# Mask matmuls behind the scores and a new split of the probability copies, in the attention stage of a two-layer trunk

## The reference, cut to what matters

```python
def sink_attend(qb, keys, values, masks, sinks):
    for kk, m in zip(keys, masks):
        s = jnp.einsum('bqhgd,bkhd->bhgqk', qb, kk).astype(jnp.float32) * scale
        if m is not None:
            s = jnp.where(m, s, -jnp.inf)
        parts.append(s)
    sink = ...                                   # one learned logit for each head
    p = jax.nn.softmax(jnp.concatenate(parts + [sink], axis=-1), axis=-1)
    ...                                          # out = sum over the parts of p @ v

def one_block(b):                                # 8 blocks of 128 queries
    qb = ...                                     # 128 queries, 16 heads of 64
    kb, vb = ...                                 # 384 keys and values around the block
    mask = (jnp.abs(qi[:, None] - offs[None, :]) <= WINDOW) & ((kpos >= 0) & (kpos < L))[None, :]
    return sink_attend(qb, (kb, k_ctx), (vb, v_ctx), (mask, None), sinks)
```

## Time and profile before

| | |
|---|---|
| median of 3 runs | 3098.88 us (3095.15 to 3099.98) |
| profiled execution, its own time | 3098.88 us |
| its span, first to last instruction | 3096.9 us |
| TensorE busy over the span | 2845.7 us (92%) |
| VectorE, ScalarE, GpSimd busy | 1610.1, 645.7, 502.0 us (52%, 21%, 16%) |
| mean granted TensorE clock | 0.960 |
| attention stage, first mask matmul to last division | 285.0 to 582.8 us |

### The profile page before, as it was taken

One profiled execution on the slowest core, in us unless ns is written; L12 is line 12 of the kernel. 1 busy time (PEld: TensorE's weight loads), 2 busy tenths in 40 slices (PEclk: granted clock), 3 DMA queues, 4 the chain that ended last, 5 costly groups with the idle time before them and its releaser, 6 DMA issues. The chain is left out here.

```text
span 3096.9 us, 40772 instructions
## 1 busy us (share of the span) xinstructions
PE 2845.7 (92%) x15266; PEld 1384.1 (45%) x15267; DVE 1610.1 (52%) x3256; ACT 645.7 (21%) x1161; POOL 502.0 (16%) x396
## 2 busy tenths in 40 slices
PE   5998999999799999999999588997999999999983
PEld 2444666544344444444443364443434444444430
DVE  3885555466545454545453355564544545454536
ACT  0112555201111121212121240011111111111110
POOL 0000000111022222222221111101222222222211
PEclk8999999999899999999999699998999999999996
DMA  9676300201499999999997522017999999998964
GB/s 351 234 257 179 145 15 15 74 28 41 183 337 345 315 299 323 313 336 334 309 315 246 188 101 81 27 48 277 317 309 329 303 349 325 311 320 259 355 202 176
DMA packets 147387, 717.87 MB, mean 232 GB/s; under 512 B 16485, under 2 KB 21989, under 8 KB 94711
## 3 DMA queue, kind: packets, MB, share of 16 engines
q1 hardware_dynamic: 104250, 556.89, 47.1%
q0 software_dynamic: 42336, 154.16, 20.1%
q10 hardware_dynamic: 608, 4.23, 0.3%
HBM read 600.35 MB, written 114.86 MB: 231 GB/s over the span
## 5 line engine op out<-in xcount | busy, mean ns | idle before, releaser
L1577 PE MATMUL exG<-ring,xT 128*32 128x512 f32 (+2 forms) x4448 | 1010.6, 596 | 8.6 <-DMA ring<-in_exp_w_up_dram 6.7
L1577 PEld LDWEIGHTS exG<-ring,xT 128*32 128x32 f32 (+2 forms) x4448 | 377.5, 138 | 623.2 <-issue 618.6
L1412 DVE COPY xT<-exX 128x512 f32<-128x512 f32 x146 | 101.0, 691 | 864.9 <-PE exX L1565 864.9
L1607 PE MATMUL exD<-ring,ex_hT 128*32 128x512 f32 (+2 forms) x2224 | 520.9, 598 | 1.4 <-ACT ex_hT L1515 1.4
L1359 POOL DMA_INDIRECT y_scratch<-ex_y,idx_out x144 | 239.1, 1660 | 559.9 <-DMA y_scratch<-ex_y,idx_out 344.5
L1348 POOL DMA_INDIRECT xg<-u_scratch,idx x146 | 145.4, 996 | 849.5 <-DVEq L1407 843.1
L1607 PEld LDWEIGHTS exD<-ring,ex_hT 128*32 128x32 f32 (+2 forms) x2224 | 181.1, 137 | 224.1 <-issue 222.2
L1418 DVE RECIPROCAL ex_e<-ex_e 128x256 f32<-128x256 f32 x144 | 252.4, 1753 | 5.0
L1520 ACT ACTIVATE ex_y<-exD,w_all 128x1024 f32<-128x1024 f32 x144 | 160.4, 1114 | 432.7 <-PE exD L1607 421.4
L1515 ACT ACTIVATE ex_hT<-exH 128x256 f32<-128x256 f32 x144 | 55.2, 383 | 878.1 <-PE exH L1595 878.1
L1384 DVE TENSOR_TENSOR hot<-place,slots 128x1024 bf16<-128x1024 f32 (+3 forms) x198 | 176.5, 915 | 4.8 <-PEq L237 3.9
(11 more groups left out here) (358 smaller groups left out, 2971.0 us busy)
## 6 DMA issues: line engine op xcount, KB each, us to landing
ring<-in_exp_w_gate_dram SPq DMA_DIRECT2D x130, 1024.0 KB
ring<-in_exp_w_up_dram SPq DMA_DIRECT2D x130, 1024.0 KB
ring<-in_exp_w_down_dram SPq DMA_DIRECT2D x130, 1024.0 KB, 7.6
ada_w<-in_w_ada_dram SPq DMA_DIRECT2D x48, 512.0 KB, 5.9
cx<-in_w_ada_dram SPq DMA_DIRECT2D x32, 512.0 KB, 4.7
y_scratch<-logits SPq DMA_DIRECT2D x4, 2304.0 KB, 13.9
w_q<-in_w_ada_dram SPq DMA_DIRECT2D x8, 1024.0 KB, 8.1
u_scratch<-u SPq DMA_DIRECT2D x16, 512.0 KB, 2.6
```

Source lines behind the costliest of these rows:

```text
L1412: dve.tensor_copy(xT[:, par, 0:KT // 2], psX[:, 0:KT // 2]).then_inc(xT_d, 1)
L1577: last = pe.matmul(psG[par][p:p + m], xT[:, par, k, p:p + m], ring[:, s % RING, 0:2, k * FF:(k + 1) * FF], start=k == 0, stop=k == KT - 1)
L1607: last = pe.matmul(psD[p:p + m, c], hT[:, k * P + p:k * P + p + m], ring[:, s % RING, 2, k * D + c * 512:k * D + (c + 1) * 512], start=k = ...
```

## The change

The mask tile keeps the two outer key blocks only (2x128 columns in place of 384). The near scores are now the first matmuls of the tile, and four mask matmuls of 128 columns are added on top of them. The mask comes from memory as float32 into the still unused `pT` buffer, and VectorE casts it to bfloat16 before the first pair. `pT` has its key blocks outside and its heads inside, and its filling is split by PSUM bank: VectorE takes the first two banks in three copies (512, 128 and 384 columns, with a new semaphore `T_next` between the first and second), ScalarE the last 256 columns.

```diff
-                mask = sb("mask", [P, NT, W], BF16)
+                mask = sb("mask", [P, NT, 2, P], BF16)
-                pT = sb("pT", [P, 2, 4, S])
+                pT = sb("pT", [P, 2, KC, 4, P])
+                maskf = pT[:].rearrange("p a j s c -> p (a j s c)")[:, 0:NT * 2 * P]
...
-                        sp.dma_start(mask[:].rearrange("p t s -> p (t s)").bitcast(mybir.dt.uint16), A["mask"]).then_inc(mask_in, 16)
+                        sp.dma_start(maskf, A["mask"]).then_inc(c_in, 16)
...
+                        dve.wait_ge(c_in, 32)
+                        dve.tensor_copy(mask[:].rearrange("p t a b -> p (t a b)"), maskf).then_inc(set_up, 1)
                         dve.tensor_copy(identb[:], ident[:]).then_inc(set_up, 1)
-                        dve.wait_ge(c_in, 16)
                         dve.tensor_scalar(nsink[:], sink[:], -1.0, None, ALU.mult).then_inc(set_up, 1)
-                        dve.wait_ge(set_up, 2)
+                        dve.wait_ge(set_up, 3)
...
-                            dve.tensor_copy(pT[:, q % 2, p % 2 * 2, 0:512], pair[p % 2][:, 0:512]).then_inc(copied_d, 1)
+                            s, at = p % 2 * 2, pair[p % 2]
+                            dve.tensor_copy(pT[:, q % 2, 0:4, s], at[:, 0:512].rearrange("p (j c) -> p j c", c=P))
+                            dve.wait_ge(T_next, p + 1)
+                            dve.tensor_copy(pT[:, q % 2, 4, s], at[:, 512:S])
+                            dve.tensor_copy(pT[:, q % 2, 0:3, s + 1], at[:, S:1024].rearrange("p (j c) -> p j c", c=P)).then_inc(copied_d, 1)
...
-                            act.activation(two[:, 512:2 * S], pair[p % 2][:, 512:2 * S], ACT.Copy).then_inc(copied_a, 1)
+                            act.activation(pT[:, q % 2, 3:KC, p % 2 * 2 + 1], pair[p % 2][:, 1024:2 * S].rearrange("p (j c) -> p j c", c=P), ACT.Copy).then_inc(copied_a, 1)
...
-                        pe.wait_ge(set_up, 1)
-                        pe.wait_ge(mask_in, 16)
+                        pe.wait_ge(set_up, 3)
...
                             for j in range(2):
-                                last = pe.matmul(sc[:, j * S:j * S + W], identb[:], mask[:, t], start=True, stop=False)
+                                last = pe.matmul(sc[:, j * S:j * S + W], q[j], near[j], start=True, stop=False)
+                            last.then_inc(near_mm, 1)
                             for j in range(2):
-                                last = pe.matmul(sc[:, j * S:j * S + W], q[j], near[j], start=False, stop=True)
-                            last.then_inc(near_mm, 1)
+                                pe.matmul(sc[:, j * S:j * S + P], identb[:], mask[:, t, 0], start=False, stop=False)
+                                pe.matmul(sc[:, j * S + 2 * P:j * S + W], identb[:], mask[:, t, 1], start=False, stop=True)
...
+                                    if j == 1 and k == 3:
+                                        last.then_inc(T_next, 1)
```

More of the change, by code:

```diff
@@ L153, in constants @@
     rope = np.concatenate([np.cos(ang), np.sin(ang) * sign], -1).astype(f)
[L155 to L159, removed]
+    gone = f(-1e30)
+    before = np.where(p[:, None] <= p[None, :], f(0), gone)
+    after = np.where(p[None, :] <= p[:, None], f(0), gone)
+    none = np.full((P, P), gone, f)
+    mask = np.stack([np.stack([none if t == 0 else before, none if t == NT - 1 else after], 1) for t in range(NT)], 1)
     a = 2 * np.pi * (np.outer(np.arange(FGW), np.arange(P + 1)) % FGW) / FGW
@@ L187, in constants @@
         "rope": rope.reshape(SEQ, 2 * HD),
-        "mask": mask.reshape(P, NT * 3 * P).astype(np.uint16),
+        "mask": mask.reshape(P, NT * 2 * P).astype(f),
         "feat": feat.reshape(FGW // P, P, FGW).transpose(1, 0, 2).reshape(P, -1).copy(),
@@ L654, in attend @@
                 prob = sb("prob", [P, 2, 2, S])
-                pT = sb("pT", [P, 2, 4, S])
+                pT = sb("pT", [P, 2, KC, 4, P])
                 zero = logits[:].rearrange("p t e -> p (t e)")
+                maskf = pT[:].rearrange("p a j s c -> p (a j s c)")[:, 0:NT * 2 * P]
                 pair = [ps(f"pair{i}", [P, 1536]) for i in range(2)]
                 psO, psR = ps("att_o", [P, 4, P]), ps("att_den", [P, 4, P])
-                c_in, mask_in, set_up, own = sem("att_in"), sem("mask_in"), sem("att_set_up"), sem("att_own")
+                c_in, set_up, own = sem("att_in"), sem("att_set_up"), sem("att_own")
                 q_in = [sem(f"q_in{i}") for i in range(2)]
@@ L662, in attend @@
                 near_mm, score_mm, max_done, exp_done = sem("near_mm"), sem("score_mm"), sem("max_done"), sem("exp_done")
-                T_first, T_rest, copied_a, copied_d, pv_mm, o_done = (sem(n) for n in (
-                    "probT_first", "probT_rest", "probT_a", "probT_d", "pv_mm", "o_done"))
+                T_first, T_next, T_rest, copied_a, copied_d, pv_mm, o_done = (sem(n) for n in (
+                    "probT_first", "probT_next", "probT_rest", "probT_a", "probT_d", "pv_mm", "o_done"))
                 sink_in, sink_done, den_own, den_done, spread_done, den_mm, share_done = (sem(n) for n in (
@@ L791, in copy @@
                             at_least(act, pv_mm, 2 * q - 2)
-                            two = pT[:, q % 2, p % 2 * 2:p % 2 * 2 + 2].rearrange("p s c -> p (s c)")
-                            act.activation(two[:, 512:2 * S], pair[p % 2][:, 512:2 * S], ACT.Copy).then_inc(copied_a, 1)
+                            act.activation(pT[:, q % 2, 3:KC, p % 2 * 2 + 1], pair[p % 2][:, 1024:2 * S].rearrange("p (j c) -> p j c", c=P), ACT.Copy).then_inc(copied_a, 1)
                         def sinks(n):
@@ L863, in values @@
                                     last = pe.matmul(psO[a * HD:(a + 1) * HD, 2 * half:2 * half + 2], v[:, slot(t, j), kv * HD:(kv + 1) * HD],
-                                                     pT[:, q % 2, 2 * a:2 * a + 2, j * P:(j + 1) * P], start=j == 0, stop=j == KC - 1)
+                                                     pT[:, q % 2, j, 2 * a:2 * a + 2], start=j == 0, stop=j == KC - 1)
                             last.then_inc(pv_mm, 1)
```

## The result

The changed kernel takes 3133.84 us (median of 4 runs, 3126.85 to 3135.49) against 3097.22 for the one before in the same comparison (4 runs, 3095.15 to 3099.98). The ratio is 1.0116, 95% interval 1.0102 to 1.0131: slower by 36.6 us, where 41.1 were forecast. The profiled execution took 3136.99 us itself and has a span of 3135.2 us, 38.3 more than before, so what is read from the two profiles comes out 2 us higher than the medians.

The account below looks back on a forecast made before the run. The prediction took a ring of scores, row maximum and VectorE's copy to bound the attention steps. Steps +36.4, start +4.0 and end +0.7 sum to 41.1 us on 3098.9, giving 3140 us; eight in ten within 3126 to 3157.

Parts of the forecast that it names:

- The bound: Attention stage: a ring of scores, row maximum and VectorE's copy bound two of four steps; after, all at 5.13 us.
- What would show it: Signs in the attention profile: maxima 5.13 us apart, first score matmul released by VectorE's third copy in nearly every step.
- The copies: VectorE's copies in the attention steps: 512 to 1024 columns in three instructions, 0.69 to 1.34 us, +0.65 a step.
- The scores: Score matmuls in the attention steps: new order and narrow masks make 1.83 us into 1.94, +0.11 a step.
- weights that are no longer loaded ahead, 0.1: Score matmuls: a weight load behind the tiling switch no longer runs ahead of its matmul, 0.1 us a step.
- ScalarE's smaller copy: Attention steps: ScalarE's copy shrinks from 768 to 256 columns, 0.81 to 0.38 us, worth nothing.
- The start: Attention stage start: TensorE waits for the larger mask load, the sinks and VectorE's cast, +4.0 us.
- The end: Attention stage end: the last pairs' three copies lie on the way to the last division, +0.7 us.
- The smaller lengthening (3126): Attention ring: tiling switches cost nothing more, saved mask columns are won, 4.91 us a step, about 3126 us; chance 0.08.
- The slower one (3158): Attention steps: joints between copies and narrow matmuls cost more, +0.91 and +0.44 at worst, about 3158 us; chance 0.10.
- The faster case: Attention steps: scores waited for ScalarE's copy, so its cut by 0.43 us helps, about 3089 us; chance 0.02.
- The falling clock: Attention stage: TensorE waits more and drops from 2.4 to 1.2 GHz in parts, 3180 us; chance 0.02.

Follow-up runs that it names:

- order alone: Kernel before with the same wide mask matmuls moved behind the near scores; 3103.99 us, ratio 1.0015.
- mirrored split: Kernel before with ScalarE copying the first two banks (1024 columns) and VectorE the last 256; 3088.71 us against 3097.94, ratio 0.9973.
- fewer values: Changed kernel without the value matmuls of the third key block; attention stage 340.3 us against 340.7, whole 3220.83 us in one run.
- two copies: Changed kernel with VectorE's 1024 columns in two copies of 512 and the old pT layout; 3128.51 us, ratio 1.0101.

## Why the prediction was right, point by point

*The bound.* Right. A ring of scores, row maximum and VectorE's copy bound two of four steps, and after the change all. The copies alone bring +31.4 us, the rest of the change +3.2, and less work for TensorE brings nothing. One sign of "What would show it" failed: the first score matmul was to wait for the third copy also in the steps with denominators, and TensorE was to wait in every step. In those steps it waits 0.03 us. The ring ends last by about 0.1 (5.04 against 4.94), and no more.

*The copies.* Forecast +0.65 a step from a copy pair elsewhere in the kernel, measured +0.67: 0.69, 0.28 and 0.55 us, starting 0.61 and 0.20 apart. By the table in the errata section of the Trainium skill ("VectorE: DVE Perf Modes") it was +0.78. The fixed part for each instruction is real (0.07 us net for the third one), but the overlap of neighbours takes back some of it, so the row was the better guide.

*The scores.* The mechanism was right, the size off: forecast +0.11 a step, measured 0.00. The passage costs its 0.1 (order alone). The term that was off is "weights that are no longer loaded ahead, 0.1": near start to transposes is 0.85 + 0.32 + 0.64 = 1.81, not 1.94. The records show an extra 0.1, which I take for such a load, once in the context scores of either order, so the 0.65 taken for them held it already. Before, it fell to the last context matmul, whose two records start 0.21 apart:

```profile
422.50 0.48 PE L839 MATMUL pair<-kT,qT_in 64*128 64x128 f32 x2
```

(One record takes 0.27.) Now it falls to the first (L841, 508.26 and 508.48), and the last has its records 0.11 apart (L844, 508.59 and 508.70). Of the two masks' saved columns the full 0.1 came. A step measures 5.035 for 5.13, 5.9 us less in 62 of them; three long steps, of which the last section tells, took 1.4 back, which leaves the miss of 4.5.

*The layout of pT.* Worth nothing, as forecast: the value matmuls span 1.08 and 1.5 us as before.

*ScalarE's smaller copy.* Worth nothing, as forecast: it ends 1.35 us ahead of VectorE's.

*The start.* +3.75 for 4.0. The cast took 1.23 for 1.31. Not foreseen: the first two pairs run 0.62 us shorter. The narrow masks are not the reason, since with the mask loaded directly, and the same masks, they take 6.37, more than the 6.26 before. What differs is when the granted clock rises. The windows from the first score matmul on, of the kernel before and of the changed one:

```profile
285.00:290.80 5.80, 5.78 (x21) 3.13 (x23) 1.82 (x3) 0.69 (x2) 0.00 (x0) 0.50 0.92 234
290.80:293.00 2.20, 1.89 (x16) 1.29 (x12) 1.69 (x3) 1.24 (x5) 0.00 (x0) 0.99 1.05 205
...
290.50:295.00 4.50, 4.50 (x18) 2.20 (x18) 1.03 (x1) 0.00 (x0) 0.00 (x0) 0.50 1.05 202
295.00:297.00 2.00, 1.46 (x15) 1.12 (x14) 1.48 (x3) 1.31 (x3) 0.00 (x0) 0.99 1.04 203
```

The clock is at 1.2 GHz (0.50) for 5.8 us of TensorE's work before, for 4.5 in the changed kernel, and for 6.6 with the mask loaded directly.

*The end.* +1.3 for 0.7. The last pair's exponentials wait for the sink term, which stands behind VectorE's longer copies, and no scores hide that: 0.65. The denominators stand behind the last pair's own copies: again 0.65. ScalarE's smaller copy takes nothing off.

*The rivals.* The smaller lengthening (3126) was half right: the narrower masks were won, but the passage cost its 0.1 as well, and the two cancel. The slower one (3158) falls: narrow masks start 0.06 apart, and the copies overlap. The faster case, that ScalarE's copy is the one waited for, falls: its cut by 0.43 us left no trace. The falling clock appeared in one short place, below.

*The size.* The sum of 41.1 is 4.8 above the 36.35 of the profiles. Start, first two pairs and even steps came out 6.8 shorter than forecast, the three long steps and the end 2.0 longer. That the two cancel in part is luck.

## What to carry to other kernels

When the profile shows an engine at over 97% busy, read the distance of the steps before believing it, and follow one step of each length to see what it waits for. Unequal steps alone prove nothing, since the mirrored split has them too (4.10, 4.52, 4.95) with hardly a wait of TensorE. Here a wait of 0.2 us in every second step gave the ring away. Find the ring, and give the engine that has a long instruction in it the small share of any divisible work. In this kernel the split by PSUM bank was worth -0.3% one way round and +1.0% the other.

## What was not expected of the hardware

TensorE's clock fell inside the stage. In the changed kernel, four stretches of the early steps (us, busy us and counts by engine, then granted clock, DMA share, GB/s):

```profile
297.00:302.00 5.00, 3.92 (x32) 2.71 (x31) 2.89 (x6) 2.28 (x7) 0.00 (x0) 1.00 1.04 209
302.00:304.20 2.20, 0.36 (x4) 0.12 (x2) 2.08 (x5) 1.69 (x4) 0.00 (x0) 1.00 1.04 199
304.20:308.80 4.60, 4.54 (x24) 3.48 (x24) 1.96 (x3) 0.35 (x2) 0.00 (x0) 0.63 1.05 204
308.80:315.00 6.20, 5.67 (x46) 3.38 (x44) 3.73 (x9) 3.54 (x10) 0.00 (x0) 1.00 1.03 361
```

The first pairs have no values yet to fill the time of the copies, so TensorE waited 1.90 us. Just after, the granted clock went from 2.4 to 1.2 GHz for part of 4.6 us, and two steps took 5.64 and 5.45. In the kernel with the copies alone one early step took 6.39, in the one with fewer values two took 5.20 and 5.47. With the mask loaded directly, and with two copies, no step did, although TensorE waited 1.90 and 1.84 us at the same place. What decides is not shown: there is one profile of each kernel, and the same wait came with the fall and without it. It was worth about 1 us. From 315 to 600 us, with waits of 0.90 us in every second step, the granted clock is 1.00.

One step later in the changed kernel took 5.39 with VectorE's first copy 0.28 us late, for no cause that the trace shows. The kernel with fewer values has 5.40 at the same pair, the others nothing. This stays open.
